# The experts' split activations stored float by float side by side, with a gap between chunks

## Chip, cores and metric

The kernel runs on one core of a Trainium2 chip. The metric is the device time of one execution in microseconds; smaller is better.

## What is computed

Two residual layers of a trunk of 256 tokens and 1024 channels. Each has three token mixers and a channel mixer. The channel mixer of layer 0 is a dense SwiGLU, that of layer 1 sends each token to two of eight experts:

```python
def swiglu(h, w1, w3, w2):
    return (silu(h @ w1) * (h @ w3)) @ w2

logits = h @ w_router                      # 256 tokens x 8 experts
top_val, top_idx = top_k(logits, 2)
gates = scatter(softmax(top_val), top_idx) # 0 for experts not chosen
for e in range(8):                         # w1, w3: 1024 x 3584, w2: 3584 x 1024
    out = out + gates[:, e:e+1] * swiglu(h, w1[e], w3[e], w2[e])
```

All inputs and the output are float32. The change touches only the experts.

## The kernel before

**Split numbers.** Each float32 operand of a large product is split in two float32r tiles: `high`, its rounded value, and `low`, the rest. A product is three matmuls (`products`, lines 267 to 273): high by high (line 270), high by low (271), low by high (272). Each matmul loads its first operand as weights (128 columns, shown as PEld) and then streams its second, the moving operand, into a PSUM bank.

**Weights from memory.** The expert matrices come in pieces of 1 MB, [128, 2048] float32, into six buffers `raw` (SyncE issues them). ScalarE makes `w_high` (line 256), VectorE `w_low` (line 260), each with three buffers. A piece's high half may be made when TensorE is through with the piece three before it; a `raw` buffer is refilled when its low half is made. In the experts the pieces are the *moving* operand, 512 columns at a time; what TensorE loads as weights are the activations.

**A job.** The experts run as jobs, one for each expert (eight here), 42 pieces each, in seven blocks of 512 hidden channels. Of the operands loaded as weights:

- `hgH`, `hgL` ([128, 8, 128]) are the halves of the rows gathered for the expert. Four gather steps on TensorE (line 1238, 8 matmuls each) put them in PSUM, and ScalarE copies each with one activation (line 527).
- `gH`, `gL` ([128, 512]) are the halves of g = silu(a) * b, transposed. `turn` transposes g (line 1254), ScalarE writes `gH` (538), VectorE `gL` as the difference (949).

For each block, TensorE runs `up` twice (lines 1242 to 1249: 24 matmuls each, with `hgH`, `hgL` as weights), with the transposes between them, and then `down` of the block before (1257 to 1267: 24 matmuls with `gH`, `gL` as weights). That is 72 matmuls a block and 504 a job. At a job's end stand the gather for the next job and the last `down`; inside the next job's first block stand `combine` (line 1271: the results' rows put back by a matmul) and `add_rows` and `make_perm` on VectorE (930, 923).

The order on each engine is written out by hand and held by semaphores. ScalarE's order in a block is three splits, `t_high`, `silu`, three splits; VectorE's is three low splits, `t_low`, one split, `mult`, two splits. `down` waits for `t_low`, and the next job's `up` for the four gather copies.

**Places.** Tiles lie one after another in each partition of SBUF. The rows of `hgH` and `hgL` that one matmul loads are 128 floats without a gap (512 bytes), those of the moving pieces 512 floats without a gap. The dense layer uses the same tiles `gH` and `gL`, there as the moving operand (line 1190), and loads `w_high` and `w_low` as weights; there `h_high` has 4 floats between its chunks (`STAGGER`).

Of the kernel before, what the change touches and what calls it, by code (L numbers as in the profile page):

```python
# [22 lines left out]
F32 = mybir.dt.float32  # L23
F32R = mybir.dt.float32r
I32 = mybir.dt.int32
U32 = mybir.dt.uint32
ALU = mybir.AluOpType
ACT = mybir.ActivationFunctionType
AX_X = mybir.AxisListType.X

P = 128
D = 1024
KC = D // P
# [18 lines left out]
SPLIT = 3  # L52
PIECE = 2048
STAGGER = 4


C_IDENT, C_HALVES, C_UPTO, C_ONES, C_AFTER, C_BEFORE, C_MASK, C_IOTA, C_POOL = range(9)
# [55 lines left out]
def trunk(nc, xt, consts, params, w_in, w_br_pool, w_br_conv, w_br_attn, w_out,  # L113
          ffn_w1, ffn_w3, ffn_w2, exp_w1, exp_w3, exp_w2, out):
    with ExitStack() as ctx:
        def sb(name, shape, dt=F32):
            return ctx.enter_context(nc.sbuf_tensor(name, shape, dt))

        def sem(name):
            return ctx.enter_context(nc.semaphore(name))  # L120

        bank = [ctx.enter_context(nc.psum_tensor(f"bank{i}", [P, 512], F32)) for i in range(8)]
# [7 lines left out]
        hf = sb("h_full", [P, KC, S])  # L130
        hH = sb("h_high", [P, KC, S + STAGGER], F32R)[:, :, 0:S]
        hL = sb("h_low", [P, KC, S], F32R)
# [43 lines left out]
        gH = sb("g_high", [P, 512], F32R)  # L176
        gL = sb("g_low", [P, 512], F32R)
        htH = sb("ht_high", [P, TT, D], F32R)
        htL = sb("ht_low", [P, TT, D], F32R)
        hgH = sb("hg_high", [P, KC, P], F32R)  # L180
        hgL = sb("hg_low", [P, KC, P], F32R)
        xacc = sb("xacc", [P, TT, D])
        ysb = sb("ysb", [P, D])
        permG = sb("perm_gated", [P, TT, P])
# [26 lines left out]
        s = {n: sem(n) for n in names}  # L211
# [11 lines left out]
        def fold(ap, k):  # L223
            return ap.rearrange("p (k n) -> p k n", k=k)
# [33 lines left out]
        def split_low(dve, c, r=0):  # L258
            dve.wait_ge(s["high_done"], num(c + 1, r))
            nc.vector.tensor_tensor(wl[c % SPLIT][:], raw[c % RAW][:], wh[c % SPLIT][:].bitcast(F32),  # L260
                                    ALU.subtract).then_inc(s["split_done"], 1)
# [90 lines left out]
        def _(act):  # L352
# [155 lines left out]
            def experts():  # L508
# [26 lines left out]

                def t_high(count):
                    act.wait_ge(s["m_t"], count)
                    nc.scalar.activation(gH[:], bank[4][:], ACT.Copy).then_inc(s["m_high"], 1)

                def silu(up_done):  # L540
                    act.wait_ge(s["used"], up_done)
# [52 lines left out]
        def _(dve):  # L594
# [7 lines left out]
            def stepped():  # L602
                dve.wait_ge(s["dve_step"], steps[0])

            def norm(nn):
                dve.wait_ge(s["norm_root"], nn + 1)
                nc.vector.reciprocal(rinv[:, 0:S], rt[:, 0:S]).then_inc(s["norm_step"], 1)  # L607
                dve.wait_ge(s["norm_step"], nn + 1)

                def low(g):  # L610
                    dve.wait_ge(s["h_high_done"], 4 * nn + g + 1)
                    nc.vector.tensor_tensor(hL[:, 2 * g:2 * g + 2, :], hf[:, 2 * g:2 * g + 2, :],  # L612
                                            hH[:, 2 * g:2 * g + 2, :].bitcast(F32),
                                            ALU.subtract).then_inc(s["h_low_done"], 1)

                for k in range(KC):
                    nc.vector.scalar_tensor_tensor(  # L617
                        out=hf[:, k, :], in0=xT[:, k, :], scalar=A(nn // 2, (A_GMIX, A_GFFN)[nn % 2] + k),
                        in1=rinv[:, 0:S], op0=ALU.mult, op1=ALU.mult).then_inc(s["norm_h"], 1)
                    if k >= 3 and k % 2:  # L620
                        low(k // 2 - 1)
                low(3)
# [309 lines left out]
            def experts():  # L932
                norm(3)
                nc.vector.memset(zero[:].bitcast(F32), 0.0).then_inc(s["zeros"], 1)
                nc.vector.memset(permT[:], 0.0).then_inc(s["m_ptout"], 1)
                route()
                split_low(dve, MOE0 + 2)
                job_table()
                stepped()
                dve.wait_ge(s["fill_act"], 12)  # L940

                def mult(count, up_done):
                    dve.wait_ge(s["used"], up_done)
                    dve.wait_ge(s["m_silu"], count)
                    nc.vector.tensor_tensor(gu[:], sl[:], bank[1][:], ALU.mult).then_inc(s["m_mult"], 1)  # L945

                def t_low(count):
                    dve.wait_ge(s["m_high"], count)
                    nc.vector.tensor_tensor(gL[:], bank[4][:], gH[:].bitcast(F32), ALU.subtract).then_inc(s["m_low"], 1)

                def job(j):
                    r0, c = j * EXP_BLOCKS, MOE0
                    for k in range(SPLIT if isinstance(j, int) else 0, 4):
                        split_low(dve, c + k, r0)
                    mult(r0 + 1, j * JOB_PIECES + (MOE0 + 4))
                    split_low(dve, c + 4, r0)
                    split_low(dve, c + 5, r0)
                    add_rows(j * 4)
                    make_perm(0, perm, j + 1)
                    make_perm(2, permG, j)  # L960
                    with dve.Fori(0, EXP_BLOCKS - 1) as i:
                        r = j * EXP_BLOCKS + i
                        split_low(dve, c + 6, r)
                        split_low(dve, c + 7, r)
                        split_low(dve, c + 8, r)
                        t_low(r + 1)
                        split_low(dve, c + 9, r)
                        mult(r + 2, r * RAW + (MOE0 + 8))
                        split_low(dve, c + 10, r)
                        split_low(dve, c + 11, r)  # L970
                    t_low(j * EXP_BLOCKS + EXP_BLOCKS)

                job(0)
                dve.wait_ge(s["jobs_ready"], 1)
                njobs = dve.value_load(jobi[0:1, 12:13], min_val=EXPERTS, max_val=EXPERTS + EXTRA_JOBS)
                with dve.Fori(1, njobs) as j:
                    job(j)
                add_rows(njobs * 4)
# [14 lines left out]
        def _(pe):  # L993
# [217 lines left out]
            def experts():  # L1211
                small_h(bank[7][:, S:2 * S], 64, 3)
                for f in range(12):
# [5 lines left out]
                    t, half_ = f % 4 // 2, f % 2  # L1219
# [37 lines left out]
                def down(c, r, count, stop=False):  # L1257
                    pe.wait_ge(s["m_low"], count)
                    for half_ in range(2):
                        H, L = take_piece(pe, c + half_, r, 2)  # L1260
                        for n in range(2):
                            ins = products(pe, bank[2 + n][:], [
                                (gH[:, (2 * half_ + k) * P:(2 * half_ + k) * P + P], gL[:, (2 * half_ + k) * P:(2 * half_ + k) * P + P],
                                 H[:, k, 512 * n:512 * n + 512], L[:, k, 512 * n:512 * n + 512]) for k in range(2)],
                                start=False, stop=stop and half_ == 1)
                        ins.then_inc(s["used"], 1)
# [131 lines left out]
```

## Time and profile before

| | |
|---|---|
| time, median of 3 | 1713.96 us (1713.95 to 1717.34) |
| profiled execution | 1714.5 us, of which 1712.4 are its span |
| TensorE matmul busy | 1662.2 us, 97% of the span |
| weight loads busy | 1444.0 us, 84% |
| VectorE busy | 1283.0 us, 75% |
| ScalarE busy | 1053.5 us, 62% |
| DMA, mean over the span | 264 GB/s |
| eight expert jobs | 1011 us, the last 59% of the span |

In a profile, PE is a matmul and PEld the weight load that goes ahead of it. A matmul's recorded length is longer than the time by which the next one follows, as they overlap in the array; so "busy" says little on TensorE, and the distance from start to start (here called the *step*) is what a matmul costs. The granted clock (PEclk) says what share of 2.4 GHz TensorE was given.

### The profile page before, as it was taken

What the parts mean: (1) busy time and instruction counts of PE and PEld (TensorE: products, weight loads), DVE (VectorE), ACT (ScalarE), POOL (GpSimd) and SP (SyncE); (2) the same over time, 40 slices, a digit from 0 to 9 for tenths busy, and PEclk for the clock granted to TensorE, in tenths of its full rate; (3) what the DMA queues carried; (4) which work ended last, traced back from release to release, by engine and by line L of the source; (5) the groups of instructions that cost most, each with busy time, mean ns of one, the idle gap of its engine ahead of it and who ended that gap; (6) DMA issues with size and microseconds to landing.
All of it is one profiled execution on the core that took longest, in us unless ns stands there. A gap on an engine that the chain in (4) does not pass through costs nothing.

```text
span 1712.4 us, 25143 instructions
## 1 busy us (share of the span) xinstructions
PE 1662.2 (97%) x9630; PEld 1444.0 (84%) x9630; DVE 1283.0 (75%) x1078; ACT 1053.5 (62%) x902; POOL 51.9 (3%) x52
## 2 busy tenths in 40 slices
PE   7999989999899998999999999999999999999998
PEld 7988889999798888788788788788788788788787
DVE  5964854454697485888887888888888888888886
ACT  5544444453544445677677677677677677677675
POOL 0131000000013100000000000000000000000000
PEclk9999999999999999999999999999999999999999
DMA  9543445555354342699899899899899899899894
GB/s 336 167 133 100 147 136 174 185 179 185 120 156 144 99 148 85 241 381 370 294 375 364 304 377 348 320 374 337 335 373 337 332 375 337 325 381 339 322 381 155
DMA packets 231292, 452.46 MB, mean 264 GB/s; under 512 B 6992, under 2 KB 80720, under 8 KB 231120
## 3 DMA queue, kind: packets, MB, share of 16 engines
q1 hardware_dynamic: 231248, 451.82, 74.2%
q8 instruction: 34, 0.56, 0.1%
q14 instruction: 10, 0.08, 0.0%
HBM read 450.74 MB, written 1.05 MB: 264 GB/s over the span
## 4 chain that ended last, share of the span: by engine, by line
PE 89%; DVE 8%; issue 2%; ACT 1%; DVEq 0%; DMA 0%; ACTq 0%
PE bank L270 27%; PE bank L271 26%; PE bank L272 26%; DVE w_low L260 3%; PE bank L1238 2%; PE bank L1254 1%; DVE xacc L930 1%; PE bank L998 1%; DVE h_full L691 1%; PE bank L1088 1%; DVE gate L686 1%; ACT w_high L256 1%; DVE h_full L617 1%; PE bank L1107 0%; DVE rinv L607 0%
## 5 line engine op out<-in xcount | busy, mean ns | idle before, releaser
L260 DVE TENSOR_TENSOR w_low<-raw,w_high 128x2048 fp32r<-128x2048 f32 x427 | 975.5, 2290 | 300.6 <-ACT w_high L256 300.0
L256 ACT ACTIVATE w_high<-raw 128x2048 fp32r<-128x2048 f32 x427 | 818.3, 1917 | 418.6 <-PE bank L272 416.0
L270 PE MATMUL bank<-w_high,hg_high 128*128 128x512 f32 x896 | 354.9, 396 | 8.8 <-DVE w_low L260 8.8
L272 PE MATMUL bank<-w_high,hg_low 128*128 128x512 f32 x896 | 349.8, 390 | 0.0
L271 PE MATMUL bank<-w_low,hg_high 128*128 128x512 f32 x896 | 349.8, 390 | 0.0
L270 PE MATMUL bank<-h_high,w_high 128*128 128x256 f32 x1056 | 304.0, 288 | 9.2 <-DVE h_low L612 4.8
L271 PE MATMUL bank<-h_low,w_high 128*128 128x256 f32 x1056 | 298.8, 283 | 0.0
L272 PE MATMUL bank<-h_high,w_low 128*128 128x256 f32 x1056 | 298.2, 282 | 0.0
L270 PEld LDWEIGHTS bank<-h_high,w_high 128*128 128x128 f32 x1056 | 200.5, 190 | 14.6 <-issue 9.4
L270 PEld LDWEIGHTS bank<-w_high,hg_high 128*128 128x128 f32 x896 | 168.8, 188 | 45.3 <-DVE w_low L260 11.0
L271 PEld LDWEIGHTS bank<-h_low,w_high 128*128 128x128 f32 x1056 | 200.4, 190 | 1.6 <-issue 1.4
L272 PEld LDWEIGHTS bank<-h_high,w_low 128*128 128x128 f32 x1056 | 200.1, 189 | 0.0
L272 PEld LDWEIGHTS bank<-w_high,hg_low 128*128 128x128 f32 x896 | 168.7, 188 | 36.3
L271 PEld LDWEIGHTS bank<-w_low,hg_high 128*128 128x128 f32 x896 | 168.8, 188 | 33.7
L270 PE MATMUL bank<-w_high,g_high 128*128 128x512 f32 x448 | 175.1, 391 | 0.0
L272 PE MATMUL bank<-w_high,g_low 128*128 128x512 f32 x448 | 174.4, 389 | 0.0
L271 PE MATMUL bank<-w_low,g_high 128*128 128x512 f32 x448 | 174.3, 389 | 0.0
L272 PEld LDWEIGHTS bank<-w_high,g_low 128*128 128x128 f32 x448 | 84.1, 188 | 17.6
L271 PEld LDWEIGHTS bank<-w_low,g_high 128*128 128x128 f32 x448 | 84.1, 188 | 17.2
L270 PEld LDWEIGHTS bank<-w_high,g_high 128*128 128x128 f32 x448 | 84.1, 188 | 17.1
L347 POOL TENSOR_SCALAR decay<-cst,fg 128x128 f32<-128x128 f32 x48 | 51.7, 1092 | 518.8 <-DVE fg L792 409.4
L945 DVE TENSOR_TENSOR gu<-sl,bank 128x512 f32<-128x512 f32 x56 | 38.2, 682 | 31.5 <-PE bank L272 31.5
(225 smaller groups left out, 1580.8 us busy)
## 6 DMA issues: line engine op xcount, KB each, us to landing
raw<-exp_w SPq DMA_DIRECT2D x336, 1024.0 KB, 5.7
raw<-w_in SPq DMA_DIRECT2D x42, 1024.0 KB, 5.2
raw<-ffn_w SPq DMA_DIRECT2D x33, 1024.0 KB, 5.3
raw<-w_out SPq DMA_DIRECT2D x8, 1024.0 KB, 5.3
raw<-w_br_attn SPq DMA_DIRECT2D x4, 1024.0 KB, 5.0
raw<-w_br_pool SPq DMA_DIRECT2D x2, 1024.0 KB, 5.2
raw<-w_br_conv SPq DMA_DIRECT2D x2, 1024.0 KB, 5.4
cst<-consts SPq DMA_DIRECT2D x1, 1280.0 KB, 13.8
```

Source lines behind the costliest of these rows:

```text
L256: nc.scalar.activation(wh[c % SPLIT][:], raw[c % RAW][:], ACT.Copy).then_inc(s["high_done"], 1)
L260: nc.vector.tensor_tensor(wl[c % SPLIT][:], raw[c % RAW][:], wh[c % SPLIT][:].bitcast(F32), ALU.subtract).then_inc(s["split_done"], 1)
L270: pe.matmul(dst, lh, rh, start=start and i == 0, stop=False)
L271: pe.matmul(dst, lh, rl, start=False, stop=False)
L272: last = pe.matmul(dst, ll, rh, start=False, stop=stop and i == len(terms) - 1)
L347: nc.gpsimd.tensor_scalar(decay[:, h % 2, k, :], C(m), lf[:, tile, h:h + 1], None, ALU.mult).then_inc(s["decays"], 1)
L617: nc.vector.scalar_tensor_tensor(out=hf[:, k, :], in0=xT[:, k, :], scalar=A(nn // 2, (A_GMIX, A_GFFN)[nn % 2] + k), in1=rinv[:, 0:S], op0= ...
L686: ins = nc.vector.scalar_tensor_tensor(out=to, in0=g, scalar=1.0, in1=fold(bank[UNIT_BANK[u]][:], 2), op0=ALU.add, op1=ALU.mult)
L691: ins = nc.vector.tensor_tensor(dst, dst, g, ALU.add)
L930: nc.vector.tensor_tensor(dst, dst, bank[b][:], ALU.add).then_inc(s["m_add"], 1)
L945: nc.vector.tensor_tensor(gu[:], sl[:], bank[1][:], ALU.mult).then_inc(s["m_mult"], 1)
L1238: ins = pe.matmul(bank[GATHER_BANKS[g]][:, k * P:k * P + P], src[:, t, ch * P:ch * P + P], perm[:, t, :], start=t == 0, stop=t == TT - 1)
```

## The change

The split tiles of the experts become two tiles with both halves in them: float 0 of the high half, float 0 of the low half, float 1 of the high half, and so on, 256 floats for a chunk of 128, and then 8 floats (32 bytes) that nothing uses. `hgH`, `hgL`, and the new `geH`, `geL` are views of them with a stride of two floats. The experts' `t_high`, `t_low`, the gather copies and `down` now use the views; the dense layer keeps `gH` and `gL`. No instruction is added, taken away or moved, and no wait.

```diff
+GAP = 8
-        hgH = sb("hg_high", [P, KC, P], F32R)
-        hgL = sb("hg_low", [P, KC, P], F32R)
+        hgX = sb("hg_halves", [P, KC, 2 * P + GAP], F32R)
+        gX = sb("g_halves", [P, 4, 2 * P + GAP], F32R)
+        hgH, hgL = (hgX[:, :, 0:2 * P].rearrange("p k (s two) -> p two k s", two=2)[:, i] for i in range(2))
+        geH, geL = (gX[:, :, 0:2 * P].rearrange("p k (s two) -> p two k s", two=2)[:, i] for i in range(2))
...
-                    nc.scalar.activation(gH[:], bank[4][:], ACT.Copy).then_inc(s["m_high"], 1)
+                    nc.scalar.activation(geH, fold(bank[4][:], 4), ACT.Copy).then_inc(s["m_high"], 1)
...
-                    nc.vector.tensor_tensor(gL[:], bank[4][:], gH[:].bitcast(F32), ALU.subtract).then_inc(s["m_low"], 1)
+                    nc.vector.tensor_tensor(geL, fold(bank[4][:], 4), geH.bitcast(F32), ALU.subtract).then_inc(s["m_low"], 1)
...
-                                (gH[:, (2 * half_ + k) * P:(2 * half_ + k) * P + P], gL[:, (2 * half_ + k) * P:(2 * half_ + k) * P + P],
+                                (geH[:, 2 * half_ + k, :], geL[:, 2 * half_ + k, :],
```

## Rows read from the trace of the kernel before

**Rows 1.** The page, its first rows: busy time of each engine, and the granted clock

```profile
PE 1662.2 (97%) x9630; PEld 1444.0 (84%) x9630; DVE 1283.0 (75%) x1078; ACT 1053.5 (62%) x902; POOL 51.9 (3%) x52
...
PEclk9999999999999999999999999999999999999999
```

**Rows 2.** Windows: seven expert jobs, then one steady block; busy us and count by engine

```profile
core 0: us, PE busy (x) PEld busy (x) DVE busy (x) ACT busy (x) POOL busy (x), PEclk, DMA share, GB/s
701.20:1588.30 887.10, 879.40 (x4034) 721.24 (x4033) 749.86 (x448) 636.52 (x441) 0.00 (x0) 1.00 0.95 348
1033.26:1050.08 16.82, 16.82 (x78) 13.91 (x77) 14.87 (x9) 12.48 (x9) 0.00 (x0) 1.00 1.00 378
```

**Rows 3.** The page, costliest groups: the splits, one matmul and one weight load of the experts

```profile
L260 DVE TENSOR_TENSOR w_low<-raw,w_high 128x2048 fp32r<-128x2048 f32 x427 | 975.5, 2290 | 300.6 <-ACT w_high L256 300.0
L256 ACT ACTIVATE w_high<-raw 128x2048 fp32r<-128x2048 f32 x427 | 818.3, 1917 | 418.6 <-PE bank L272 416.0
L270 PE MATMUL bank<-w_high,hg_high 128*128 128x512 f32 x896 | 354.9, 396 | 8.8 <-DVE w_low L260 8.8
...
L270 PEld LDWEIGHTS bank<-w_high,hg_high 128*128 128x128 f32 x896 | 168.8, 188 | 45.3 <-DVE w_low L260 11.0
```

**Rows 4.** Timeline of TensorE: start us, length us; 24 matmuls of one down step

```profile
1004.97 0.39 PE L270 MATMUL bank<-w_high,g_high 128*128 128x512 f32 x1
...
1010.41 0.39 PE L270 MATMUL bank<-w_high,hg_high 128*128 128x512 f32 x1
```

**Rows 5.** Timeline of TensorE in the dense layer: first and last of 45 steps, 256 columns

```profile
430.92 0.28 PE L272 MATMUL bank<-g_high,w_low 128*128 128x256 f32 x1
...
436.31 0.28 PE L272 MATMUL bank<-g_high,w_low 128*128 128x256 f32 x1
```

**Rows 6.** Timeline of TensorE's weight loads in combine: float32 streams of 512 columns

```profile
1082.28 0.19 PEld L1271 LDWEIGHTS bank<-ysb,perm_t 128*128 128x128 f32 x1 [0.24 <-issue]
...
1083.99 0.19 PEld L1271 LDWEIGHTS bank<-ysb,perm_t 128*128 128x128 f32 x1 [0.24 <-issue]
```

**Rows 7.** Timeline of TensorE: the gather, 32 matmuls of 128 columns from first row to last

```profile
1061.22 1.98 PE L1238 MATMUL bank<-perm,ht_high 128*128 128x128 f32 x16
...
1064.82 0.41 PE L1310 MATMUL bank<-cst,perm_gated 128*128 128x128 f32 x2
```

**Rows 8.** Timeline of TensorE after a transpose: first and last of 8 steps

```profile
1016.52 0.40 PE L271 MATMUL bank<-w_low,hg_high 128*128 128x512 f32 x1
...
1018.38 0.39 PE L270 MATMUL bank<-w_high,hg_high 128*128 128x512 f32 x1
```

**Rows 9.** Timeline of TensorE: two places with h_high and its 16 spare bytes as moving operand

```profile
275.66 0.29 PE L270 MATMUL bank<-h_high,w_high 128*128 128x256 f32 x1
275.79 0.29 PE L271 MATMUL bank<-h_low,w_high 128*128 128x256 f32 x1
...
660.80 0.28 PE L271 MATMUL bank<-h_low,w_high 128*128 128x256 f32 x1
660.91 0.28 PE L272 MATMUL bank<-h_high,w_low 128*128 128x256 f32 x1
```

**Rows 10.** Timeline of ScalarE, VectorE and TensorE at a job's end and start

```profile
1065.02 0.60 ACT L527 ACTIVATE hg_low<-bank 128x512 fp32r<-128x512 f32 x1 [0.30 <-PE bank L1238]
...
1067.73 4.53 DVE L260 TENSOR_TENSOR w_low<-raw,w_high 128x2048 fp32r<-128x2048 f32 x2 [4.55 <-ACT w_high L256]
...
1070.54 0.39 PE L270 MATMUL bank<-w_high,hg_high 128*128 128x512 f32 x1
...
1086.71 2.48 DVE L930 TENSOR_TENSOR xacc<-xacc,bank 128x512 f32<-128x512 f32 x4
...
1092.47 0.50 PE L270 MATMUL bank<-w_high,hg_high 128*128 128x512 f32 x1 [1.11 <-DVE w_low L260]
```

**Rows 11.** Window of the DMA in steady blocks (last columns: clock, DMA share, GB/s)

```profile
1030.00:1040.00 10.00, 10.00 (x48) 8.26 (x47) 8.82 (x5) 7.92 (x6) 0.00 (x0) 1.00 1.05 388
```

## The prediction

> **What bounds the kernel now.** The first rows of the page come first: TensorE is busy 97% of the span, at a granted clock of ten tenths, so at its upper level of 2.4 GHz [rows 1]. The chain that ended last says the same, but neither tells what a matmul costs. For that I read windows. Seven expert jobs last 887.1 us, so 126.7 us each, and a block in the middle of one lasts 16.82 us, filled by 72 matmuls of 512 columns and four transposes; VectorE has 14.87 us of work in it and ScalarE 12.48 [rows 2]. The groups show that ScalarE and VectorE mostly wait for TensorE, and TensorE for VectorE's `w_low` rarely (8.8 us in all) [rows 3]. So in the experts, 59% of the span, the distance from one matmul's start to the next (the step) sets the time, and the timeline gives it: 24 steps take 1010.41 - 1004.97 = 5.44 us, 226.7 ns each [rows 4]. A job has 504 of them, 114.3 of its 126.7 us.
>
> **What the step is made of.** In the dense layer, the same kind of matmul with 256 columns takes 5.39 us for 45 steps, 119.8 ns each [rows 5]. 256 columns more cost 106.9 ns, so 0.417 ns a column, one tick of 2.4 GHz. 512 columns are then 213.3 ns, and what is left is 13.4 ns with 512 columns and 13.1 with 256. This rest doesn't grow with the stream, so it belongs to the weight load beside it, or to the change from one matmul to the next. It isn't a fixed price of the change: in combine, float32 streams of 512 columns run at half the pace (426.7 ns) and 4 steps take 1.71 us, 427.5 each, a rest of 1 ns, give or take 3 by the rounding [rows 6]. It isn't constant either: after a transpose, the first 8 steps take 1.86 us, 232.5 ns each, with the same instructions [rows 8]; and where the moving operand is `h_high` with its 16 spare bytes, steps of 0.13 and of 0.11 us stand beside each other [rows 9]. The rest thus depends on how two reads of SBUF lie against each other: the full-rate stream, and the load of 128 weights. That load alone takes at most 112.5 ns (the gather's 32 matmuls of 128 columns in 3.60 us, where the stream is only 53 ns) [rows 7]: it walks through memory at about half the pace of the stream. Where both go at one pace (rows 6, both at half), the rest is nearly gone.
>
> **The change, part by part.** No instruction and no wait is added or moved. What changes is how three kinds of instruction walk through SBUF.
>
> *The weight loads* (4032 in the experts) now take every second float. If the load keeps its time of 188 ns as recorded [rows 3], it passes 1024 bytes in place of 512 in that time, and goes through memory at the pace of the full-rate stream, as in rows 6. The gap moves the load by 32 bytes against the stream from chunk to chunk, so that no one bad position holds for all chunks. I expect the rest to fall. Its lower end is the 1 ns of rows 6; its upper end, for this case, 9 ns. I take 5 ns: the gather's step is 112.5 where its 128 floats at half pace take 106.7, a rest of 5.8 [rows 7], and the least step with `h_high`, 0.11 us, is a rest of some 3 [rows 9]. Step 218.3 ns, saving 8.4 ns.
>
> In each job 24 of the 504 give nothing: the `up` that runs while VectorE is in `add_rows`, permutations and a split. TensorE waits 1.11 us behind it for `w_low` [rows 10], and that chain starts at the end of the piece before, so the wait grows by what `up` saves. 480 x 8.4 ns = 4.03 us a job, 32.3 us for eight.
>
> *The copies* (`t_high`, the gather copies on ScalarE, `t_low` on VectorE) now write with a stride, and `t_low` also reads with one. No row shows a strided write of this size. Element count and engines stay, so a gain is excluded; the bounds are nothing and twice today's time. Twice would cost `t_low` some 0.7 us a block, inside VectorE's idle 16.82 - 14.87 = 1.95 us [rows 2], 1.35 us after the change. It would show at a job's end: the last gather copy starts at 1065.02, the split behind it lets VectorE begin at 1067.73, its first piece (2.29 us) is there at 1070.02, and TensorE starts on it at 1070.54 [rows 3, 10]. Four copies at 1.2 us in place of 0.6, of which the gather steps hide a part, come 1.5 to 1.9 us later against 0.5 us of cover: up to 1.4 us a job, 11 us in all. I take nothing, since the rows nearest to it give the time by elements; 11 us stays in the range.
>
> *What comes late next.* A block would last 16.82 - 72 x 0.0084 = 16.22 us. Splits: ScalarE starts a split when a piece is used, 1.92 + 2.29 us later both halves are there [rows 3], and TensorE needs them after two more pieces, 24 x 0.218 = 5.24 us; that still holds. DMA: a block takes six pieces, 6.29 MB, so 388 GB/s, and the rows show 388 held over 10 us at full share [rows 11]. So the DMA has no room left inside a run of blocks, but six buffers and the stalls at each job's end, over which the mean is now 348 GB/s [rows 2] and would be 359. I charge nothing and keep 0 to 5 us for the range.
>
> *The sum.* The profiled execution took 1714.5 us, 0.5 over the median. 1714 - 32.3 gives 1682 us. With a rest of 1 ns the saving is 12.4 x 3840 = 47.6 us, so 1666; with 9 ns, 16.9 us, so 1697.
>
> The Trainium skill (TensorE: Matmul & The Clock Gate, Back-to-back issue gap) gives a warm step as columns over 2.4 GHz and 2.5 ns more, 215.8 ns for 512. This trace doesn't agree as it stands, 226.7 ns [rows 4]; if the change brought the step there, the saving would be an estimated 10.9 x 3840 = 42 us and the time 1672.
>
> **Rivals.**
>
> *The rest goes by the memory passed over (slower).* The rest is about 13.3 ns for 512 bytes of weights, with 256 and with 512 columns alike [rows 4, 5]. If every stretch of memory that the load touches costs the stream its bit, twice the stretch costs twice: rest 26.7, step 240. That is 13.3 x 504 = 6.7 us a job, less 0.3 in the wait of rows 10, and 51 us in all: 1765; with half of it 1740. It decides as soon as the load's doubled footprint isn't matched by fewer meetings. For it speaks that the rest equals so exactly a fixed sum per load; against it, that steps vary with position [rows 8, 9] and that rows 6, with loads of the same size, show no rest; though there the stream goes at half pace and may have room to give way.
>
> The Trainium skill (SBUF — State Buffer, Specifications) says that SBUF is read in lines of 16 bytes, and that at least two hits a line are needed for full bandwidth. Every second float is just two hits, so by that rule the load itself keeps its time; but it opens 64 lines in place of 32, which is this rival if each opening costs the stream. No row here shows a load with a stride.
>
> *Only the pattern is shuffled.* The rest depends on position alone, not on pace, and the new places give now a better and now a worse one. The bad end is the 232.5 ns of rows 8, 5.8 more than now over all 4032 matmuls, 1737; on the good side I take half of that, 2.9 x 3840 = 11 us, 1703; the likeliest is where it is now, 1714. This is also the case in which the change doesn't do what it says.
>
> *The load gets slower.* At twice its time it would take up to 225 ns and stand beside a step of 226.7: it decides only from there. With a rest on top, 230 ns and 1727; with the strided copies, some more.
>
> **How the numbers follow.** The rest falls: 0.50, 1666 to 1698, forecast 1682. The pattern is shuffled: 0.22, of which faster 0.08, the same 0.07, slower 0.07. The memory passed over: 0.21. The load or the copies get slower: 0.07, of which 0.01 comes out the same. This kernel's measurement tells 0.2%, about 3.4 us, from no change. Faster 0.58, the same 0.08, slower 0.34. The likeliest case's own range is 1666 to 1698; to leave out no more than 2 in 10, the range goes up through the shuffled and slowed cases to the near end of the footprint case: 1666 to 1745.
>
> **What would show it.** Right: the matmuls of lines 270 to 272 with `hg` and `g` start 216 to 222 ns apart, the weight loads still record 188 ns, a job lasts 122.7 us, the wait for `w_low` in each job grows from 1.1 to 1.3 us, and the mixer and the dense layer are as they were. Footprint: steps of 235 to 240, with loads of 188. Slower load: PEld of lines 270 to 272 at 290 ns. Copies: lines 527 and 538 over 0.6 us, line 949 over 0.68, and TensorE waiting at a job's start. What would make the forecast wrong without any of these is the DMA: TensorE's rows would wait for `w_low` inside a job's run of blocks.

## The result, and the profile after

| | before | after |
|---|---|---|
| time, median of 3 | 1713.96 us | 1731.12 us (1730.92 to 1731.26) |
| span of the profiled execution | 1712.4 us | 1729.2 us |
| start of the seven jobs of [rows 2] in it | 701.2 us | 701.9 us |
| one expert job | 126.73 us | 128.78 us |
| one block of 72 matmuls and 4 transposes | 16.82 us | 17.12 us |
| step of a matmul in the experts, mean | 227.3 ns | 231.7 ns |

The changed kernel takes 1.0095 times as long, with an interval of 1.0075 to 1.0114: some 16 us slower (17.2 between the medians), where 32 us less were forecast. The page of the changed kernel, its first rows and two of its groups (the code is three lines longer, so line 270 of before is line 273 here):

```profile
PE 1681.0 (97%) x9630; PEld 1474.2 (85%) x9630; DVE 1283.5 (74%) x1078; ACT 1056.4 (61%) x902; POOL 52.0 (3%) x52
...
PEclk9999999999999998999999999999999999999999
...
L273 PE MATMUL bank<-w_high,hg_halves 128*128 128x512 f32 x896 | 358.5, 400 | 7.7 <-DVE w_low L263 7.7
...
L273 PEld LDWEIGHTS bank<-w_high,hg_halves 128*128 128x128 f32 x896 | 175.4, 196 | 40.9 <-DVE w_low L263 9.8
```

The same instructions in the same numbers. TensorE has 19 us more of busy time, VectorE 0.5, ScalarE 3. The weight load of the experts is recorded with 196 ns (188 before, [rows 3]), the matmul with 400 (396). The clock is full in the seven jobs of the window. The one lower digit stands for 648 to 692 us, up to the first expert matmuls, and a window around it has a clock of 0.89 in both kernels; the first nine expert matmuls still follow each other at 427 ns, half the clock, in both. The windows of the changed kernel answer to [rows 2, 11]: seven jobs, a steady block, and ten us inside blocks (columns as there).

```profile
701.90:1603.34 901.44, 894.70 (x4034) 746.57 (x4033) 750.15 (x448) 638.63 (x441) 0.00 (x0) 1.00 0.94 342
1038.59:1055.71 17.12, 17.12 (x77) 14.42 (x76) 14.87 (x9) 12.52 (x8) 0.00 (x0) 1.00 1.01 373
1030.00:1040.00 10.00, 10.00 (x47) 8.40 (x46) 8.57 (x4) 6.97 (x4) 0.00 (x0) 1.00 1.01 355
```

Seven jobs take 901.44 in place of 887.10 us, 2.05 us more each, so 16.4 us for eight; 0.7 us more stand ahead of the window. Half of these fall before the first expert matmul (688.77 for 688.46 us), the rest between it and the window, in the first 48 expert matmuls. A block takes 0.30 us more, 4.2 ns for each of its 72 matmuls, and 504 x 4.2 = 2.1 us is the whole of a job's growth. So in the jobs the step is what has changed. TensorE's timeline in a `down`, the 24 steps that answer to [rows 4], from the first start to the 25th:

```profile
1010.36 0.39 PE L273 MATMUL bank<-w_high,g_halves 128*128 128x512 f32 x1
...
1015.91 0.39 PE L273 MATMUL bank<-w_high,hg_halves 128*128 128x512 f32 x1
```

5.55 us, 231.3 ns a step. The steps are also unlike each other now. Before, the trace has 226 or 227 ns for each of these 24; after, they go from 226 to 236 ns, and from block to block nearly the same uneven row comes back. Last, the copies and a job's start and end, the changed kernel's timeline of ScalarE and then of TensorE ([rows 10]):

```profile
1067.90 0.64 ACT L541 ACTIVATE g_halves<-bank 128x512 fp32r<-128x512 f32 x1 [1.29 <-PE bank L1257]
1068.74 0.65 ACT L530 ACTIVATE hg_halves<-bank 128x512 fp32r<-128x512 f32 x1 [0.20 <-PE bank L1241]
...
1071.43 0.64 ACT L530 ACTIVATE hg_halves<-bank 128x512 fp32r<-128x512 f32 x1 [0.27 <-PE bank L1241]
```

```profile
1077.05 0.39 PE L273 MATMUL bank<-w_high,hg_halves 128*128 128x512 f32 x1
...
1099.22 0.50 PE L273 MATMUL bank<-w_high,hg_halves 128*128 128x512 f32 x1 [0.97 <-DVE w_low L263]
```

A gather copy takes 0.64 us in place of 0.60, and TensorE starts on the new rows 5.62 us after the last copy began; before it was 5.52 [rows 10]. No wait stands there. The wait for `w_low` later in the job is 0.97 us (1.11 before).

### The profile page after: what moved, and what is told of

Same layout as the page of the kernel before. It is cut to its first block, busy times and chain, and to the rows that moved or that the text cites. A ratio compares the mean times of both kernels' runs of the same rounds, so it can differ in the third digit from the quotient of the medians.

```text
span 1729.2 us, 25143 instructions
## 1 busy us (share of the span) xinstructions
PE 1681.0 (97%) x9630; PEld 1474.2 (85%) x9630; DVE 1283.5 (74%) x1078; ACT 1056.4 (61%) x902; POOL 52.0 (3%) x52
## 4 chain that ended last, share of the span: by engine, by line
PE 89%; DVE 7%; issue 2%; ACT 1%; DVEq 0%; DMA 0%; ACTq 0%
PE bank L273 27%; PE bank L275 27%; PE bank L274 27%; DVE w_low L263 3%; PE bank L1241 2%; PE bank L1257 1%; DVE xacc L933 1%; PE bank L1001 1%; DVE h_full L694 1%; PE bank L1091 1%; DVE gate L689 1%; DVE h_full L620 0%; PE bank L1110 0%; ACT w_high L259 0%; DVE rinv L610 0%
## 5 line engine op out<-in xcount | busy, mean ns | idle before, releaser
L273 PE MATMUL bank<-w_high,hg_halves 128*128 128x512 f32 x896 | 358.5, 400 | 7.7 <-DVE w_low L263 7.7
L275 PE MATMUL bank<-w_high,hg_halves 128*128 128x512 f32 x896 | 354.0, 395 | 0.0
L274 PE MATMUL bank<-w_low,hg_halves 128*128 128x512 f32 x896 | 352.6, 394 | 0.0
L273 PEld LDWEIGHTS bank<-w_high,hg_halves 128*128 128x128 f32 x896 | 175.4, 196 | 40.9 <-DVE w_low L263 9.8
L275 PEld LDWEIGHTS bank<-w_high,hg_halves 128*128 128x128 f32 x896 | 175.0, 195 | 34.0
L274 PEld LDWEIGHTS bank<-w_low,hg_halves 128*128 128x128 f32 x896 | 174.8, 195 | 31.9
L273 PE MATMUL bank<-w_high,g_halves 128*128 128x512 f32 x448 | 176.8, 395 | 0.0
L275 PE MATMUL bank<-w_high,g_halves 128*128 128x512 f32 x448 | 176.7, 394 | 0.0
L274 PE MATMUL bank<-w_low,g_halves 128*128 128x512 f32 x448 | 175.8, 392 | 0.0
L275 PEld LDWEIGHTS bank<-w_high,g_halves 128*128 128x128 f32 x448 | 87.4, 195 | 16.2
L273 PEld LDWEIGHTS bank<-w_high,g_halves 128*128 128x128 f32 x448 | 87.7, 196 | 15.6
L274 PEld LDWEIGHTS bank<-w_low,g_halves 128*128 128x128 f32 x448 | 87.2, 195 | 16.1
```

What stands on the lines that cost most here:

```text
L273: pe.matmul(dst, lh, rh, start=start and i == 0, stop=False)
L274: pe.matmul(dst, lh, rl, start=False, stop=False)
L275: last = pe.matmul(dst, ll, rh, start=False, stop=stop and i == len(terms) - 1)
```

## The experiments

The question was what makes the step: the doubled stretch that a load passes over, its stride, the gap, or only where the tiles come to lie. In what follows, the *distance* of a load is the start of the loaded piece less the start of the stream, in floats, with multiples of 64 floats (256 bytes) taken away. By the sizes of the tiles in the code, each weight piece and each expert tile of the kernel before starts at the same place in a period of 64 floats, so each of its loads in the experts has distance 0. Where h is the stream and is moved in place of the load (256 columns, from the small kernel in the real order on), the number given is counted the other way round, from the load to the stream.

**One stream, one load, 80 places.** 36 matmuls of 512 columns for each (stride, offset) of the loaded piece, with a matmul of 128 columns between two places:

```python
w = wts[:, at:at + P * step]
if step > 1:
    w = w.rearrange("p (s g) -> p s g", g=step)[:, :, 0]
for i in range(N_EACH):
    pe.matmul(bank[n % 7][:], w, mov[:, 0:512], start=i == 0, stop=i == N_EACH - 1)
```

> A program of matmuls alone; the trunk is left out, the output is the input. 80 layouts of the weight operand, 36 matmuls each of 128x512 float32r on one fixed moving operand: 32 places 16 bytes apart with stride one, the same 32 with stride two, then strides 3, 4, 8 and places further off. If only the place matters (position theory), the step varies with the place at stride one between some 216 and 236 ns, with a mean near the 231 ns of the changed kernel, and stride two has the same mean. If the memory passed over matters (footprint theory), stride one is near 227 ns at every place and stride two near 231 or more at every place, and strides 4 and 8 are slower still. If neither, all 80 layouts agree within 2 ns, and what makes the difference is outside TensorE.

The windows of this kernel that span the last 12 steps at a place, in this order: stride 1 with distances 0, 4, 36, 44; stride 2 with 0 and 16; strides 4 and 8 with 0.

```profile
16.09:18.81 2.72, 2.72 (x13) 2.25 (x12) 0.00 (x0) 0.00 (x0) 1.00 0.00 0
24.52:27.32 2.80, 2.80 (x14) 2.27 (x12) 0.00 (x0) 0.00 (x0) 1.00 0.00 0
92.39:95.11 2.72, 2.72 (x13) 2.25 (x12) 0.00 (x0) 0.00 (x0) 1.00 0.00 0
109.27:112.03 2.76, 2.76 (x14) 2.25 (x13) 0.00 (x0) 0.00 (x0) 1.00 0.00 0
286.58:289.41 2.83, 2.83 (x14) 2.36 (x12) 0.00 (x0) 0.00 (x0) 1.00 0.00 0
320.48:323.24 2.76, 2.76 (x14) 2.33 (x12) 0.00 (x0) 0.00 (x0) 1.00 0.02 6
617.60:620.41 2.81, 2.81 (x13) 2.81 (x13) 0.00 (x0) 0.00 (x0) 1.00 0.00 0
635.15:638.08 2.93, 2.93 (x13) 2.93 (x13) 0.00 (x0) 0.00 (x0) 1.00 0.00 0
```

The first number behind the window is the time of twelve steps: 226.7 ns each, 233.3, 226.7, 230.0; 235.6 and 230.0; 234.9 and 244.4. With stride 1 the step settles after a few matmuls, and where it settles repeats with 64 floats: 226.7 at distances 0, 36 and 60 (and at 64, 100, 124, 128, 256 and 512), 228.8 to 234.6 at the other 13 multiples of four, mostly 233.3. No settled step is below 226.7. With stride 2 it lies between 230.0 and 235.6, and doesn't always come back after 256 bytes: 0, 64, 128 and 256 floats give 235.6, 233.3, 235.5 and 233.3. The third number is the loads' busy time: 12 loads take 2.25 us with stride 1, 2.33 to 2.36 with stride 2, 188 against 196 ns. With stride 4 the loads are busy through the whole window.

So stride 2 leaves the load its pace but gives the stream nothing back, and distance 0, where the kernel before stands, is among the three best of sixteen.

**The parts one by one, in the trunk.** The gap alone, with the halves in tiles of their own:

```diff
+GAP = 8
-        hgH = sb("hg_high", [P, KC, P], F32R)
-        hgL = sb("hg_low", [P, KC, P], F32R)
+        hgH = sb("hg_high", [P, KC, P + GAP], F32R)[:, :, 0:P]
+        hgL = sb("hg_low", [P, KC, P + GAP], F32R)[:, :, 0:P]
+        geH = sb("ge_high", [P, 4, P + GAP], F32R)[:, :, 0:P]
+        geL = sb("ge_low", [P, 4, P + GAP], F32R)[:, :, 0:P]
...
```

The lines left out let `t_high`, `t_low` and `down` use `geH` and `geL`, as in the change.

> The kernel before with the halves in tiles of their own, read with stride one, and only the 32 bytes between chunks added. Position theory: the lock at 226.7 ns is lost by the gap alone, steps vary from 224 to 236 with a mean of 231, and the time is that of the changed kernel, about 1731 us. Footprint theory: steps stay at 226.7 ns, 1714 us.

The halves side by side without the gap (the changed kernel with `GAP = 0`):

> The changed kernel with the halves side by side, float by float, and no gap between chunks. Position theory: chunks are again 1024 bytes apart, the steps settle on one value as before, 226.7 ns, 1714 us. Footprint theory: stride two costs what it costs in the changed kernel, steps of 231 ns, 1731 us.

24 steps of a `down`, first start to 25th, the timeline of the gap alone and then of the halves side by side without the gap:

```profile
1008.93 0.39 PE L273 MATMUL bank<-w_high,ge_high 128*128 128x512 f32 x1
...
1014.49 0.39 PE L273 MATMUL bank<-w_high,hg_high 128*128 128x512 f32 x1
```

```profile
1011.36 0.39 PE L273 MATMUL bank<-w_high,g_halves 128*128 128x512 f32 x1
...
1016.96 0.39 PE L273 MATMUL bank<-w_high,hg_halves 128*128 128x512 f32 x1
```

The gap alone: 231.7 ns a step, uneven as in the changed kernel, 1732.85 us, 1.011 times before (1.0093 to 1.0127). Side by side without it: 233.3 ns, all 24 steps alike, 1741.01 us, 1.0159 times (1.0142 to 1.0176). There the theory of positions had expected a return to 226.7 ns and 1714 us, and missed: the steps settle on one value, but on another one, as stride 2 has a map of its own. The footprint theory, with 231 ns and 1731 us, missed too. The gap alone costs as much as the whole change, the interleaving alone more. Costs of a gap and of a stride would add up; these don't.

**A shift alone.** Tiles as before, no stride, no gap; the four expert tiles begin 32 bytes further, so that every load has distance 8:

```diff
+GAP = 8
+        shift = sb("shift", [P, GAP])
         hgH = sb("hg_high", [P, KC, P], F32R)
         hgL = sb("hg_low", [P, KC, P], F32R)
+        geH = sb("ge_high", [P, 4, P], F32R)[:, :, 0:P]
+        geL = sb("ge_low", [P, 4, P], F32R)[:, :, 0:P]
+        unshift = sb("unshift", [P, 64 - GAP])
...
```

`unshift` puts the tiles behind them back to their old places modulo 256 bytes.

> The kernel before with its contiguous halves, no gap and no stride, but the experts' four tiles 32 bytes further in SBUF. Position theory: all steps in the experts settle on 233.3 ns, the value of the map at a distance of 8 floats, 6.6 ns x 4032 = 27 us slower than before, 1740 us. If it is the gap between chunks that matters and not the place as such: no change, 1714 us.

```profile
1011.60 0.40 PE L275 MATMUL bank<-w_high,ge_high 128*128 128x512 f32 x1
...
1017.20 0.40 PE L275 MATMUL bank<-w_high,hg_high 128*128 128x512 f32 x1
```

That timeline gives 233.3 ns, and the time is 1736.84 us, 1.0123 times before (1.0106 to 1.014). 32 bytes of shift, which change no instruction's shape, cost more than the change under study.

**A gap that moves nothing.** The rival that a gap of any size costs is met by one of 64 floats, 256 bytes, on the gathered rows:

```diff
+GAP = 64
-        hgH = sb("hg_high", [P, KC, P], F32R)
-        hgL = sb("hg_low", [P, KC, P], F32R)
+        hgH = sb("hg_high", [P, KC, P + GAP], F32R)[:, :, 0:P]
+        hgL = sb("hg_low", [P, KC, P + GAP], F32R)[:, :, 0:P]
```

> The kernel before, with 64 spare floats (256 bytes) behind each 128-float chunk of the gathered rows' halves, not side by side; g as before. Theory of positions (what counts is where the loaded piece starts in a period of 64 floats, against the stream): 256 bytes move nothing, steps stay at 226.7 ns, 1714 to 1715 us. Rival (any gap between the chunks costs, since 32 bytes of it gave 231.8 ns): 2600 steps on the gathered rows by some 4.2 ns more, 1725 us.

And the halves side by side, without the gap, at the start that was best for stride 2; against the layout side by side (`GAP = 0`) the edit is:

```diff
+        shift = sb("shift", [P, 16])
         hgX = sb("hg_halves", [P, KC, 2 * P + GAP], F32R)
         gX = sb("g_halves", [P, 4, 2 * P + GAP], F32R)
+        unshift = sb("unshift", [P, 48])
```

> Halves side by side without gaps, as the kernel of 1741 us, but both tiles begin 16 floats (64 bytes) further. Theory of positions: of the starts measured with side-by-side halves this was the best (230.0 ns, against 233.3 and more at distance 0), so some 3960 steps fall from 234.1 to 230 to 231 ns: 1725 to 1729 us. Rival (the step of two floats sets the pace, the start does not): 1741 us again.

24 steps in the timeline of the one and of the other:

```profile
1004.98 0.39 PE L271 MATMUL bank<-w_high,g_high 128*128 128x512 f32 x1
...
1010.42 0.39 PE L271 MATMUL bank<-w_high,hg_high 128*128 128x512 f32 x1
```

```profile
1010.92 0.39 PE L275 MATMUL bank<-w_high,g_halves 128*128 128x512 f32 x1
...
1016.44 0.39 PE L275 MATMUL bank<-w_high,hg_halves 128*128 128x512 f32 x1
```

With 256 bytes of gap: 226.7 ns, 1714.76 us beside 1714.75, ratio 1.0001 (0.9992 to 1.0011). Side by side and moved by 64 bytes: 230.0 ns, 1727.81 us, ratio 1.0072 (1.0052 to 1.0092); 13 us better than the same layout unmoved. Both as the theory of positions had it, and both against their rivals. Against the changed kernel the moved layout can't be told apart by the times, as the intervals overlap.

**More places, other widths.** 143 more places, with streams of 256 to 512 columns, odd offsets, the stream moved in place of the load, and a load that reads one float 128 times.

> Matmuls alone again, the trunk left out; 30 matmuls for each layout. 64 places of the weights one float apart with streams of 256 columns; places that are not whole 16 bytes with 512 columns; places of the stream in place of the weights'; strides 2, 4, 8 with 256 columns; one weight float read 128 times; streams of 320, 384 and 448 columns. Position theory: the step follows the distance between stream and weights, repeats each 256 bytes, moving the stream by +n does what moving the weights by -n does, and settles on few values; some place with 256 columns gives less than the 120 ns of the dense layer. Footprint theory: the layout with one weight float read 128 times has next to no rest, 215 ns, and places matter little.

Windows of the last 12 steps: 256 columns at distances 16 and 35, 256 columns with a load of stride 4, 512 columns with a load of one single float, and 384 columns.

```profile
71.84:73.20 1.36, 1.36 (x15) 1.36 (x13) 0.00 (x0) 0.00 (x0) 1.00 0.00 0
141.54:142.98 1.44, 1.44 (x15) 1.44 (x13) 0.00 (x0) 0.00 (x0) 1.00 0.05 11
708.29:711.09 2.80, 2.80 (x13) 2.80 (x13) 0.00 (x0) 0.00 (x0) 1.00 0.00 0
722.74:725.52 2.78, 2.78 (x14) 2.27 (x13) 0.00 (x0) 0.00 (x0) 1.00 0.00 0
732.34:734.42 2.08, 2.08 (x13) 2.08 (x13) 0.00 (x0) 0.00 (x0) 1.00 0.00 0
```

113.3, 120.0, 233.3, 231.7 and 173.3 ns. A load of one single float, which passes over next to no memory, still stands beside a step of 231.7 (215 was expected if the memory passed over were the cause), so the cost isn't that of memory passed over: that rival falls. With 256 columns the same load stands at 113.3, the least. 256 columns with stride 1 settle at 113.3 ns for a few distances and at 115 to 122 for the rest. That is a possible gain for the mixers and the dense layer, which stand at 118.5. One expectation missed here: to move the stream by +n floats doesn't do what moving the load by -n does. With 512 columns and the stream moved by 4, 16 and 28 the steps are 231.7, 233.3 and 231.2 ns, where the load at the same distances (60, 48 and 36) stood at 226.7, 228.8 and 226.7.

**The real order.** The same with the three matmuls of `products` in their order, once as in the mixers and the dense layer (256 columns, chunks of h as the stream) and once as in the experts.

> Matmuls alone, the trunk left out, but in the kernel's own order of three (high by high, high by low, low by high) with operands that change from chunk to chunk. Each layout twice over: a unit of 48 matmuls with 256 columns at 33 places, with and without a gap in the rows of the stream; an up step of 24 matmuls of 512 columns with the weights' gap, place and stride as in before (gap 0), as in the changed kernel (stride 2, gap 8) and each part alone. Position theory: up settles on 226.7 with no gap, on 233.3 when all is 32 bytes further, and varies with a mean of 231 to 233 with a gap of 8 at either stride; some place of the unit settles on 113.3 ns, 120.0 being that of no distance. If what the kernel shows is due to the engines beside TensorE, up is the same in all of them.

Windows of this kernel: first 48 steps of 256 columns at distances 0 and 28; then 24 steps of 512 columns laid out as before, with the gap alone, with the shift by 8, and side by side moved by 16.

```profile
22.15:27.91 5.76, 5.76 (x50) 5.76 (x49) 0.00 (x0) 0.00 (x0) 1.00 0.01 3
102.27:107.71 5.44, 5.44 (x50) 5.44 (x49) 0.00 (x0) 0.00 (x0) 1.00 0.00 0
399.77:405.21 5.44, 5.44 (x26) 4.50 (x24) 0.00 (x0) 0.00 (x0) 1.00 0.00 0
410.91:416.46 5.55, 5.55 (x25) 4.50 (x24) 0.00 (x0) 0.00 (x0) 1.00 0.01 3
422.16:427.76 5.60, 5.60 (x25) 4.51 (x24) 0.00 (x0) 0.00 (x0) 1.00 0.00 0
545.70:551.22 5.52, 5.52 (x25) 4.66 (x24) 0.00 (x0) 0.00 (x0) 1.00 0.00 0
```

The trunk's values are those of the `down` above, the means those of all plain steps of the experts.

| layout of the experts' loads | this kernel, ns | trunk, ns | mean over the jobs, ns | ratio of times |
|---|---|---|---|---|
| before | 226.7 | 226.7 | 227.3 | 1 |
| gap of 256 bytes on `hg` | not run | 226.7 | 227.3 | 1.0001 |
| side by side, moved by 16 | 230.0 | 230.0 | 230.2 | 1.0072 |
| changed: side by side, gap 8 | 231.7 | 231.3 | 231.7 | 1.0095 |
| gap of 8 alone | 231.4 | 231.7 | 231.8 | 1.011 |
| shift by 8 alone | 233.3 | 233.3 | 233.2 | 1.0123 |
| side by side alone | 233.3 | 233.3 | 234.1 | 1.0159 |

A kernel with nothing but matmuls gives the trunk's step within 0.4 ns, so in these layouts neither the copies nor the transfers beside it play a part. And the ratio follows from the step within 3 us: 4032 matmuls by 231.7 - 227.3 = 4.4 ns are 17.7 us for the changed kernel (16.3 measured), by 5.9 ns 23.8 us for the shift (21.1), by 6.8 ns 27.4 us for the last row (27.3).

But the map of one stream and one load doesn't carry over place by place: at stride 1 and without a gap, distance 36 stands at 233.3 in this order and 60 at 228.3, both 226.7 before, and distance 4 at 226.7, where it was 233.3. Distances 0, 8 and 16 agree.

**The other side of the trunk: h without its spare bytes.** The kernel before has 16 spare bytes in `h_high` between chunks. Without them the chunks of `h_high` are all at distance 0 from the weight pieces, and `h_low`, 128 bytes nearer, is at distance 0 too; the tiles behind stay in place:

```diff
-        hH = sb("h_high", [P, KC, S + STAGGER], F32R)[:, :, 0:S]
+        hH = sb("h_high", [P, KC, S], F32R)
         hL = sb("h_low", [P, KC, S], F32R)
+        keep = sb("keep", [P, 32])
```

> The kernel before without the 16 bytes between the chunks of h_high; all tiles behind it stay where they are. Position theory: with every chunk at a distance of 0 or 32 floats, the mixers' and the dense layer's 256-column steps settle, h_high on 120.0; they were 118.6 to 119.5 in the mean, so about 1 ns x 3168 = 3 us slower, 1717 us; the experts keep 226.7 ns.

1720.49 us, 1.0032 times before (1.0021 to 1.0044). The some 3370 steps of 256 columns with h that nothing interrupts rise from 118.5 to 119.9 ns in the mean, 4.7 us of the 5.5; the direction was expected, with 3 us.

**h at a better distance.** In the real order the small kernel had 113.3 ns with the stream 28, 36 or 48 floats behind the load. Both halves in one tile, 28 floats further, without the spare bytes; nothing of the experts is touched:

```diff
-STAGGER = 4
+AT = 28
-        hH = sb("h_high", [P, KC, S + STAGGER], F32R)[:, :, 0:S]
-        hL = sb("h_low", [P, KC, S], F32R)
+        both = sb("h_halves", [P, AT + 2 * KC * S], F32R)
+        hH, hL = (both[:, AT + i * KC * S:AT + (i + 1) * KC * S].rearrange("p (k s) -> p k s", k=KC) for i in range(2))
```

> The kernel before, but the halves of the normalized rows h lie in one tile and begin 28 floats (112 bytes) behind the place at distance 0 from the weight pieces, without the 16 spare bytes between chunks. Nothing of the experts is touched. Theory of positions, carried to the 256-column products: at distance 28 the small kernel settled at 113.3 ns a matmul after some 8 of them; in the kernel before, 3375 such steps take 118.5 ns. 3375 by 5 ns is 17 us less: 1697 us, up to 1704 if every new tile must settle again. Rival (in the real kernel the copies and transfers beside it shake the pattern off): 1713 to 1720 us.

The same with `AT = 36`, and a spare tile further on that brings the experts' tiles back to their distance:

> As the kernel with distance 28, but with distance 36, where the small kernel was at 113.3 ns from the second matmul on; the experts' tiles are put back to their old distance. Theory of positions: 1695 to 1700 us, at or below the time with distance 28. Rival as there: 1713 to 1720 us.

95 steps of an `up` in the dense layer, first and last matmul: without the spare bytes, with 28, with 36.

```profile
308.43 0.28 PE L271 MATMUL bank<-h_high,w_high 128*128 128x256 f32 x1
...
319.83 0.28 PE L273 MATMUL bank<-h_high,w_low 128*128 128x256 f32 x1
```

```profile
303.11 0.28 PE L270 MATMUL bank<-h_halves,w_high 128*128 128x256 f32 x1
...
313.94 0.28 PE L272 MATMUL bank<-h_halves,w_low 128*128 128x256 f32 x1
```

```profile
306.72 0.28 PE L271 MATMUL bank<-h_halves,w_high 128*128 128x256 f32 x1
...
318.00 0.28 PE L273 MATMUL bank<-h_halves,w_low 128*128 128x256 f32 x1
```

120.0, 114.0 and 118.7 ns. With 28 floats the kernel takes 1703.61 us, 0.9933 times before (0.9917 to 0.995): faster than both kernels, only by where h lies. The mean of the plain steps with h falls from 118.5 to 114.7 ns, 3375 x 3.8 = 12.8 us; the experts begin 11.1 us earlier and then run as before. The forecast of 1697 had taken 113.3 for all, and 1704 if each new tile must settle again; so it is, as after an interruption up to a dozen steps of 114 to 122 ns stand before the pattern is found. With 36 floats it takes 1714.82 us, ratio 1.0 (0.999 to 1.0009), mean step 118.5: the forecast of 1695 to 1700 fails, though the small kernel had shown 113.3 there. (In this kernel the mixers' tiles of y lie 32 bytes further too; their some 370 steps go from 117.8 to 119.9 ns, 0.8 us.)

**Why 36 failed, and whether distance is all.**

> A small kernel of its own; it computes nothing of the trunk and passes its input through in place of the output. Its question is whether the step hangs on the distance between stream and loaded piece or on each one's own place, and why distance 36 settled at 113.3 ns in the small kernel and not in the trunk. 512 columns, stream and load both moved by 4 to 48 floats: if the distance alone counts, all eight settle at 226.7 ns like distance 0; if each one's place counts, some stand at 230 to 234. 256 columns, distance 28 with both moved: 113.3 ns each by the first theory, 116 to 120 for some by the second. 256 columns with the spacing of the high and low tiles as in the trunk (6144 floats for the weights, 2048 for h) and as in the earlier small kernel: if the spacing is what the earlier one lacked, distance 36 settles at some 118 ns with the trunk's spacing and at 113.3 with its own, and distance 28 at 113.3 with both; if neither changes, what the trunk adds (copies and transfers beside, products in between) is left.

Windows of 36 steps: 512 columns with stream and load both moved by 4, 8 and 28 floats; 256 columns at distance 28 and at 36, spaced as in the trunk; distance 28 with both moved by 8 and by 36; distance 36 with both moved by 8.

```profile
34.58:42.98 8.40, 8.40 (x37) 6.77 (x36) 0.00 (x0) 0.00 (x0) 1.00 0.01 2
45.83:53.99 8.16, 8.16 (x38) 6.76 (x36) 0.00 (x0) 0.00 (x0) 1.00 0.00 0
67.86:76.14 8.28, 8.28 (x38) 6.75 (x37) 0.00 (x0) 0.00 (x0) 1.00 0.00 0
216.74:220.82 4.08, 4.08 (x38) 4.08 (x37) 0.00 (x0) 0.00 (x0) 1.00 0.01 4
284.21:288.41 4.20, 4.20 (x39) 4.20 (x37) 0.00 (x0) 0.00 (x0) 1.00 0.00 0
318.32:322.40 4.08, 4.08 (x38) 4.08 (x37) 0.00 (x0) 0.00 (x0) 1.00 0.00 0
351.79:356.11 4.32, 4.32 (x39) 4.32 (x38) 0.00 (x0) 0.00 (x0) 1.00 0.02 4
374.97:379.24 4.27, 4.27 (x39) 4.27 (x37) 0.00 (x0) 0.00 (x0) 1.00 0.00 0
```

233.3, 226.7, 230.0; 113.3, 116.7, 113.3, 120.0; 118.6 ns. Moved together by 8, 16, 32 or 48 floats, stream and load keep the step of distance 0; by 4, 28 or 36 they lose it. With 256 columns and distance 28 it is alike: kept with 8, 16 and 32, lost with 4 and 36. So the theory in its plain form, that the distance alone counts, is wrong. For these two layouts a common move by whole 32 bytes changes nothing; that isn't general, as distance 36 with both moved by 8, 16 or 32 floats stands at 118.6 in place of 116.7. The spacing of the high and low tiles plays no part (six spacings, the same step each time), so that isn't what set distance 36 apart. But distance 36 itself settles at 116.7 here and at 113.3 in the two small kernels before, with the same places modulo 256 bytes. There the second matmul had started 166 ns after the first, here 169. The trunk's 118.7 at distance 36 is the third value: its timeline goes through the same uneven row, 118, 118, 122, 121, 115, 117 ns and so on, that the small kernel settles in when both are moved by 8, 16 or 32. So the miss needs no copies or transfers beside TensorE; matmuls alone make this step too. By the sizes of the tiles the trunk's places are those that gave 116.7, not the moved ones. So a place seems to have more than one pattern, and the way into it may choose; that is argued and not tested, and why 36 has several and 28, met in three small kernels with entries of 168 to 170 ns, gave one alone stays open.

## Why the prediction was wrong

**What bounds the kernel** was right: the step in the experts. So was the accounting that turns a step into a time, as the table above shows.

**What the step is made of.** "The rest depends on how two reads of SBUF lie against each other" was right as far as it goes: where the two lie decides the step, though no run shows by what mechanism. But 13.4 and 13.1 ns for 512 and 256 columns [rows 4, 5] were no sum of their own: 256 columns go down to 113.3, a rest of 6.7, and most steps that settle on one value stand at rests of 6.7, 13.3 or 20.0 ns, 16 ticks of 2.4 GHz apart. Between them lie averages of rows of several steps, and a few even steps (116.7, 231.2).

**The step that failed** is the one on the weight loads: that a load which keeps its time but passes twice the memory "goes through memory at the pace of the full-rate stream, as in rows 6", so that the rest falls to 5 ns and the step to 218.3. The load did nearly keep its time, 188 and then 196 ns; the rest didn't fall but rose, to 231.3 - 213.3 = 18.0 ns in the `down` above. The analogy with float32 in [rows 6] was the error. Equal pace doesn't bring the rest down, since at full rate stride 2 gave 230.0 to 235.6 in every one of its places, and the single float 231.7. That rows 6 show no rest because a stream at half the rate has room is likely, but not shown. The pace itself was taken from two different times: 1024 bytes in the recorded 188 ns are 5.4 bytes a ns, where the stream passes 2048 bytes in 213.3 ns, 9.6; only with the gather's 112.5 ns, an upper bound, are the two near each other (9.1). The second half of the sentence, that the gap spreads the load over positions so that "no one bad position holds for all chunks", had it the wrong way round: no bad position held before. Distance 0 was one of the best three of sixteen in the first map and at the least step, 226.7, in the real order, and the spread took it away. As far as the record shows, the kernel before stood there by the luck of its tile sizes.

**The rivals.** "Only the pattern is shuffled" is what happened, and its bad end, 5.8 ns a step and 1737 us, was near: 4.4 ns. What was wrong was its weight (0.22) and its nearly equal sides. The rows had a hint: 24 steps all alike at 226.7 [rows 4], against 232.5 after a disturbance [rows 8]. The steady value below the disturbed one is what a lucky position looks like, and from 226.7, the least of the map, a shuffle can only lose. It isn't a shuffle alone, though: stride 2 has no place below 230 in the map. "The memory passed over" fell with the single float. "The load gets slower" didn't decide: 8 ns more on the load, still 35 ns short of the step.

The Trainium skill (SBUF — State Buffer, Specifications) asks for two hits in a line of 16 bytes for full bandwidth. The trace agrees: every second float keeps the load at 196 ns, while with every fourth the 256-column step goes from 120 to 233.3 ns, so that the load, busy through the whole window, sets the step. The Trainium skill (TensorE: Matmul & The Clock Gate, Step-by-step: what each phase is for) says that stream and load have read ports of their own, and that the load steals no read bandwidth from the running matmul. The measurements differ: 32 bytes of shift in the loaded tile make every step 6.6 ns longer. The Trainium skill (TensorE: Matmul & The Clock Gate, Back-to-back issue gap) gives, by its formula, 215.8 ns for 512 columns; no place in any run here settled below 226.7.

**The smaller terms.** ScalarE's copies took 6 to 7% more (in the mean `t_high` 620 in place of 579 ns, the gather copies 635 in place of 597), `t_low` 684 ns as before; not nothing but far from twice, and hidden as assumed. The wait for `w_low` fell to 0.97 us where 1.3 was forecast, as it must when `up` gets longer and not shorter. The DMA was never asked: a steady block has 373 in place of 378 GB/s, as it lasts longer. (The windows of ten us, 355 and 388, cut the blocks at other places.) The mixers and the dense layer were as they were (118.5 ns for the steps with h in both); the first expert matmul starts 0.3 us later, and the cause of that wasn't sought. The measured 1731.12 lay inside the range, by a rival's bounds and not by the forecast's.

## What to carry to other kernels

Where weight loads run beside full-rate float32r streams, look at the step in ns before changing a layout: a step that is the same in every matmul has found a pattern, good or bad, and any shift of a tile that isn't a multiple of 256 bytes (spare floats, a new tile allocated ahead) can lose it. So tile addresses belong to what is held fixed when two versions are compared, and a small kernel that sweeps the start over 64 floats in the real order of matmuls names the places worth trying in one run; here one such move gained 0.7%, though of two places tried only one carried over. The order matters: a sweep with one load and one stream gave other places than the three matmuls of the real kernel.

## What was not expected of the hardware

- The step of a matmul with a weight load beside it depends on where the loaded piece starts against the stream, and at stride 1 it comes back after 256 bytes: 226.7 to 237 ns for 512 columns, 113.3 to 122 for 256.
- Steps that settle on one value do so mostly at values 6.7 ns apart: 113.3 and 120.0; 226.7 and 233.3.
- For equal distances the step also depends on where both lie: distance 0 gives 226.7 ns with 512 columns, and 233.3 with both moved by 16 bytes; and at distance 36 with 256 columns it settles at 113.3, 116.7 or 118.6 in different runs and places.
- A load with a stride of two floats is recorded with 196 ns in place of 188; with a stride of four or eight floats the 256-column step is 233.3 or 241.7 ns.
- A load that reads one float 128 times leaves the 512-column step at 231.7 ns, and the 256-column step at 113.3.
- Writing every second float costs ScalarE 6 to 7% on 512 elements, and VectorE, which also reads that way, nothing.
